# Two transformer blocks on one core: the first weight unit and x in two halves, constant matmuls at the start, one semaphore set for three FFNs

## The reference, cut to what matters

```python
def rms_norm(x, g):            # eps 1e-6
    return x * rsqrt(mean(x * x, axis=-1) + eps) * g

x = x + 0.5 * swiglu(rms_norm(x, ffn1_norm), ffn1_gate, ffn1_up, ffn1_down)
# swiglu(h, g, u, d) = (silu(h @ g) * (h @ u)) @ d, hidden width 2816
```

## Time and profile before

| | us |
|---|---|
| three runs | 1970.55, 1967.21, 1971.44 |
| their median | 1970.55 |
| the profiled execution | 1967.05 |
| its span, first to last instruction | 1965.3 |
| PE busy | 1926.3 |
| PE at the start of unit 0, of unit 2 | 14.27, 41.40 |

### The profile page before, as it was taken

One profiled execution on the slowest core, in us unless ns is written; L12 is line 12 of the kernel. 1 busy time (PEld: TensorE's weight loads), 2 busy tenths in 40 slices (PEclk: granted clock), 3 DMA queues, 4 the chain that ended last, 5 costly groups with the idle time before them and its releaser, 6 DMA issues.

```text
span 1965.3 us, 24117 instructions
## 1 busy us (share of the span) xinstructions
PE 1926.3 (98%) x9630; PEld 1558.6 (79%) x9630; DVE 907.5 (46%) x1182; ACT 705.2 (36%) x957; POOL 177.3 (9%) x150
## 2 busy tenths in 40 slices
PE   8999999999999999999999999999999979999998
PEld 6888888887778898888888878777677858888887
DVE  5444422447685654644442246343546454444313
ACT  5222221354534443423231143334545353222212
POOL 2000000204430200200000032000000030000000
PEclk9999999999999999999999999999999989999999
DMA  5333322332214223333323222221212313333322
GB/s 161 97 99 93 104 89 88 104 107 66 65 44 151 92 87 100 86 107 86 106 87 105 85 89 86 65 65 44 77 53 86 99 52 102 91 105 87 104 89 75
DMA packets 213697, 175.79 MB, mean 89 GB/s; under 512 B 6565, under 2 KB 201210, under 8 KB 213626
## 3 DMA queue, kind: packets, MB, share of 16 engines
q1 hardware_dynamic: 212928, 174.74, 29.0%
q10 hardware_dynamic: 698, 0.05, 0.0%
HBM read 172.67 MB, written 2.10 MB: 89 GB/s over the span
## 4 chain that ended last, share of the span: by engine, by line
PE 89%; DVE 4%; ACT 3%; POOL 2%; DMA 1%; issue 1%; SPq 0%; DVEq 0%; POOLq 0%; ACTq 0%
PE bank L484 25%; PE bank L486 24%; PE bank L485 24%; PE bank L658 6%; PE bank L531 2%; PE bank L951 1%; PE bank L532 1%; PE bank L533 1%; PE bank L920 1%; ACT w_hi L1049 1%; DVE w_lo L1511 1%; DMA w_raw<-in_w_in 1%; DVE n_lo L1520 1%; PE bank L935 1%; POOL hgrn_suffix L442 1%
## 5 line engine op out<-in xcount | busy, mean ns | idle before, releaser
L484 PE MATMUL bank<-n_hi,w_hi 128*128 128x512 f32 x1760 | 707.4, 402 | 18.5 <-DVE n_lo L1520 10.2
L1511 DVE TENSOR_TENSOR w_lo<-w_raw,w_hi 128x2048 fp32r<-128x2048 f32 x160 | 369.2, 2307 | 753.0 <-ACT w_hi L1049 752.9
L486 PE MATMUL bank<-n_hi,w_lo 128*128 128x512 f32 x1760 | 690.2, 392 | 0.0
L485 PE MATMUL bank<-n_lo,w_hi 128*128 128x512 f32 x1760 | 690.1, 392 | 0.0
L1049 ACT CAST w_hi<-w_raw 128x2048 fp32r<-128x2048 f32 x160 | 305.4, 1909 | 610.9 <-PE bank L486 526.0
L484 PEld LDWEIGHTS bank<-n_hi,w_hi 128*128 128x128 f32 x1760 | 332.9, 189 | 105.0 <-issue 23.6
L486 PEld LDWEIGHTS bank<-n_hi,w_lo 128*128 128x128 f32 x1760 | 333.0, 189 | 71.1
L485 PEld LDWEIGHTS bank<-n_lo,w_hi 128*128 128x128 f32 x1760 | 333.3, 189 | 67.6 <-issue 2.6
L425 POOL TENSOR_TENSOR sum_squares<-sum_squares,sq 128x512 f32<-128x512 f32 x42 | 66.0, 1571 | 933.2 <-ACT sq L1064 928.8
L484 PE MATMUL bank<-h_hi,w_hi 128*128 (+1 forms) x352 | 139.2, 396 | 0.0
L486 PE MATMUL bank<-h_hi,w_lo 128*128 (+1 forms) x352 | 139.1, 395 | 0.0
(11 more groups left out here) (306 smaller groups left out, 1954.6 us busy)
## 6 DMA issues: line engine op xcount, KB each, us to landing
w_raw<-in_w_in SPq DMA_DIRECT2D x68, 512.0 KB, 4.6
w_raw<-in_ffn_gate SPq DMA_DIRECT2D x44, 512.0 KB, 4.0
w_raw<-in_ffn_up SPq DMA_DIRECT2D x44, 512.0 KB, 5.2
w_raw<-in_ffn_down SPq DMA_DIRECT2D x44, 512.0 KB, 3.9
w_raw<-in_w_gate SPq DMA_DIRECT2D x22, 512.0 KB, 4.0
w_raw<-in_w_up SPq DMA_DIRECT2D x22, 512.0 KB, 5.2
w_raw<-in_w_down SPq DMA_DIRECT2D x22, 512.0 KB, 4.0
w_raw<-in_w_kv_mem SPq DMA_DIRECT2D x16, 512.0 KB, 4.5
```

Source lines behind the costliest of these rows:

```text
L484: pe.matmul(acc, w_hi, x_hi, start=start, stop=False)
L485: pe.matmul(acc, w_hi, x_lo, start=False, stop=False)
L486: return pe.matmul(acc, w_lo, x_hi, start=False, stop=stop)
L1511: dve.tensor_tensor(wlo[par][:, :], raw[par][:, :], whi[par][:, :].bitcast(F32), ALU.subtract).then_inc(w_lo_ready, 1)
```

## The change

What it does, all at the start except the last point:

- **Loads.** `x` comes in eight pieces (128 tokens by one half of the model dimension, 256 KB) and unit 0 in four (gate or up, four k chunks, 256 KB), each with its own semaphore. The order on SP: three pieces of the first half of `x`, gate, the fourth piece, up; then four pieces of the second half, gate, up. Then unit 1 as before.
- **Turning.** `turn_in(0)` turns chunks 0 to 3 into banks 4 to 7, `turn_in(1)` chunks 4 to 7 into banks 2 to 5; the two that reuse banks 4 and 5 wait for the copies of `x` out of them. `turn_in(1)` stands in PE's list behind unit 0's third k chunk.
- **Constant matmuls.** `warm(n)` multiplies ones by the identity into bank 0: six calls at the start, three behind the gain's transpose, three behind each of the four pieces of the first half.
- **Products.** Unit 0 goes k chunk by k chunk, gate then up, not all of gate first.
- **Splits.** ACT and DVE split unit 0 in four pieces of 512 columns, placed between the `n_hi` and `n_lo` of each half. DVE copies chunks 0 and 1 of `x` after four `n_lo`, the other six after all eight.
- **The sum.** In the first FFN the matmul that sums the squares stands behind unit 1's sixth k chunk, not its second.
- **Semaphores.** The three FFNs share six semaphores that count on (`h0` = 22 f is added to what is waited for), instead of six each.

```diff
+X_BANK = (4, 5, 6, 7, 2, 3, 4, 5)
@@ SP
-            for i in range(TT):
-                sp.dma_start(x_tok[:, i, :], xv[:, i, :]).then_inc(x_loaded[i], 16)
+            def load_first(half, g):
+                k0, at0 = 4 * half, (C * g + 4 * half) * P
+                sp.dma_start(raw[0][:, at0:at0 + 4 * P].rearrange("p (k n) -> p k n", k=4),
+                             first[g][:, k0:k0 + 4, 0:P]).then_inc(first_loaded[half][g], 16)
+
+            for half in range(2):
+                cols = slice(D // 2 * half, D // 2 * half + D // 2)
+                for i in range(TT):
+                    if i == TT - 1 and half == 0:
+                        load_first(half, 0)
+                    sp.dma_start(x_tok[:, i, cols], xv[:, i, cols]).then_inc(x_loaded[half][i], 16)
+                if half:
+                    load_first(half, 0)
+                load_first(half, 1)
@@ PE
-                    for g in range(2):
-                        if g == 0:
-                            pe.wait_ge(first_lo, 1)
-                        else:
-                            pe.wait_ge(w_lo_ready, 1)
-                        pe.wait_ge(x_ready, g + 1)
-                        for k in range(C):
-                            if g == 0:
-                                pe.wait_ge(n_ready, k + 1)
+                    for k in range(C):
+                        pe.wait_ge(n_ready, k + 1)
+                        for g in range(2):
+                            if k in (0, 4):
+                                pe.wait_ge(*((w_lo_ready, 1) if k and g else (first_lo, k // 2 + g + 1)))
...
+                        if k == 2:
+                            turn_in(1)
...
-                        else {1: lambda: sum_over_partitions(sums)})
+                        else {5 if f == 0 else 1: lambda: sum_over_partitions(sums)})
...
+            def warm(n):
+
+                for _ in range(n):
+                    pe.matmul(bank[0][:, 0:P], ones[:, :], ident[:, :], start=True, stop=True)
+
+            def turn_in(half):
+
+                for i in range(TT):
+                    pe.wait_ge(x_loaded[half][i], 16)
+                    for c in range(4 * half, 4 * half + 4):
+                        if i == 0 and c == 4:
+                            pe.wait_ge(gain1_ready, 1)
+                        if i == 0 and c > 5:
+                            pe.wait_ge(x_ready, c - 5)
+                        mm = pe.transpose(bank[X_BANK[c]][:, i * P:(i + 1) * P], x_tok[:, i, c * P:(c + 1) * P], ident[:, :])
+                        if i == TT - 1:
+                            mm.then_inc(x_turned, 1)
+                    if half == 0:
+                        warm(3)
+
             pe.wait_ge(ident_steps, 2)
+            warm(6)
             pe.wait_ge(gain1_loaded, 16)
...
+            warm(3)
+            turn_in(0)
@@ ACT
-            act.copy(whi[0][:, 0:W // 2], raw[0][:, 0:W // 2]).then_inc(first_hi, 1)
-            for c in range(C):
-                act.wait_ge(x_turned, c + 1)
-                act.activation(nhi[:, c, :], bank[c][:, :], ACT.Copy, scale=gain("ffn1_norm", c)).then_inc(n_hi_ready, 1)
-            act.wait_ge(w_loaded[0], 16)
-            act.copy(whi[0][:, W // 2:W], raw[0][:, W // 2:W]).then_inc(w_hi_ready, 1)
+            for half in range(2):
+                if half == 0:
+                    first_split(0, 0)
+                for c in range(4 * half, 4 * half + 4):
+                    if c in (1, 5):
+                        first_split(half, 1)
+                    act.wait_ge(x_turned, c + 1)
+                    act.activation(nhi[:, c, :], bank[X_BANK[c]][:, :], ACT.Copy, scale=gain("ffn1_norm", c)).then_inc(n_hi_ready, 1)
+                if half == 0:
+                    first_split(1, 0)
@@ DVE
+            for half in range(2):
+                if half == 0:
+                    first_split(0, 0)
+                for c in range(4 * half, 4 * half + 4):
+                    dve.wait_ge(n_hi_ready, c + 1)
+                    dve.scalar_tensor_tensor(nlo[:, c, :], bank[X_BANK[c]][:, :], gain("ffn1_norm", c), nhi[:, c, :].bitcast(F32),
+                                             ALU.mult, ALU.subtract).then_inc(n_ready, 1)
+                    if c in (0, 4):
+                        first_split(half, 1)
+                if half == 0:
+                    for c in range(2):
+                        keep_x(c)
+                    first_split(1, 0)
             for c in range(2, C):
-                dve.tensor_copy(x[:, c, :], bank[c][:, :]).then_inc(x_ready, 1)
+                keep_x(c)
             split_unit(1)
```

More of the change, by code:

```diff
@@ L233, in two_blocks @@
         unit_done = sem("unit_done")
-        x_loaded = [sem(f"x_loaded{i}") for i in range(TT)]
-        first_loaded, first_hi, first_lo = sem("first_loaded"), sem("first_hi"), sem("first_lo")
+        x_loaded = [[sem(f"x_loaded{half}_{i}") for i in range(TT)] for half in range(2)]
+        first_loaded = [[sem(f"first_loaded{half}_{g}") for g in range(2)] for half in range(2)]
+        first_hi, first_lo = sem("first_hi"), sem("first_lo")
         gain1_loaded, gains_loaded, taps_loaded = sem("gain1_loaded"), sem("gains_loaded"), sem("taps_loaded")
@@ L338, in gate_up @@
                     cols = bass.ds(n * P, P)
-                    load(par, [((0, W // 2, C), g[:, :, cols]), ((W // 2, W, C), p_[:, :, cols])],
-                         first_loaded if base == 0 and isinstance(n, int) and n == 0 else None)
+                    load(par, [((0, W // 2, C), g[:, :, cols]), ((W // 2, W, C), p_[:, :, cols])])
                 def down_pair(par, half, n):
@@ L345, in down_pair @@
                                ((W // 2, W, 1), d[:, bass.ds(2 * n + 1, 1), :])])
-                for j in range(2):
+                for j in range(1 if base == 0 else 0, 2):
                     gate_up((base + j) % 2, (base + j) // 2, j, base > 0)
@@ L676, in ffn_products @@
                     down(b + n, n, (b + n) % 2, last=(n == DOWN_UNITS - 1))
+            def warm(n):
[14 more added lines that the diff above has]
+                        warm(3)
             pe.wait_ge(ident_steps, 2)
+            warm(6)
             pe.wait_ge(gain1_loaded, 16)
-            pe.transpose(bank[7][:, 0:C], gain_rows[0:C, :], ident[0:C, 0:C]).then_inc(gain1_t, 1)
-            for i in range(TT):
-                pe.wait_ge(x_loaded[i], 16)
-                for c in range(C):
[L685 to L689, removed]
+            pe.transpose(bank[2][:, 0:C], gain_rows[0:C, :], ident[0:C, 0:C]).then_inc(gain1_t, 1)
+            warm(3)
+            turn_in(0)
             ffn_products(0, U_FFN1, N_FFN1, S_FFN1)
@@ L1043, in split @@
             def split(par, half, first=False):
-                act.wait_ge(w_loaded[par], 32 * half + (32 if par else 16))
+                act.wait_ge(w_loaded[par], 32 * half + (32 if par else 0))
                 if not first:
@@ L1146, in _, with first_split @@
             act.dma_start(convw[:, :, :], a["conv_w"][0].rearrange("(c p) j -> p c j", p=P)).then_inc(taps_loaded, 16)
+            def first_split(half, g):
+                cols = slice((C * g + 4 * half) * P, (C * g + 4 * half + 4) * P)
+                act.wait_ge(first_loaded[half][g], 16)
+                act.copy(whi[0][:, cols], raw[0][:, cols]).then_inc(w_hi_ready if half and g else first_hi, 1)
             act.wait_ge(gain1_ready, 1)
-            act.wait_ge(first_loaded, 16)
-            act.copy(whi[0][:, 0:W // 2], raw[0][:, 0:W // 2]).then_inc(first_hi, 1)
-            for c in range(C):
-                act.wait_ge(x_turned, c + 1)
-                act.activation(nhi[:, c, :], bank[c][:, :], ACT.Copy, scale=gain("ffn1_norm", c)).then_inc(n_hi_ready, 1)
-            act.wait_ge(w_loaded[0], 16)
-            act.copy(whi[0][:, W // 2:W], raw[0][:, W // 2:W]).then_inc(w_hi_ready, 1)
+            for half in range(2):
[8 more added lines that the diff above has]
+                    first_split(1, 0)
             split_unit(1)
@@ L1493, in _ @@
                     else:
[L1494 removed]
+                        act.wait_ge(down_done, 2 * (C - 1) + i + 1)
                     if i:
@@ L1616, in _, with first_split @@
-            dve.wait_ge(w_hi_ready, 1)
-            dve.tensor_tensor(wlo[0][:, W // 2:W], raw[0][:, W // 2:W], whi[0][:, W // 2:W].bitcast(F32),
-                              ALU.subtract).then_inc(w_lo_ready, 1)
+            def first_split(half, g):
+                cols = slice((C * g + 4 * half) * P, (C * g + 4 * half + 4) * P)
+                dve.wait_ge(*((w_hi_ready, 1) if half and g else (first_hi, 2 * half + g + 1)))
+                dve.tensor_tensor(wlo[0][:, cols], raw[0][:, cols], whi[0][:, cols].bitcast(F32),
+                                  ALU.subtract).then_inc(w_lo_ready if half and g else first_lo, 1)
```

70 lines of the change are left out of this document (31 added, 39 removed).

## The result

| | before | after |
|---|---|---|
| median, us (17 runs each) | 1967.21 | 1973.80 |
| lowest and highest, us | 1965.1, 1971.44 | 1970.99, 1976.03 |
| span of the profiled execution, us | 1965.3 | 1972.0 |

The ratio of after to before is 1.0029, with a 95% interval of 1.0022 to 1.0037: the change makes the kernel 0.29% slower, 5.7 us. The medians of all runs are further apart (6.6 us), the spans of the two profiles too (6.7); both still lie inside the interval, which is 4.3 to 7.3 us.

The account below looks back on a forecast made before the run. The PE's own work was taken to fill nine tenths of the span; unit 2's start 3.9 us later plus a second clock fall of 1.7 made 5.6, added to 1970.55 for 1976.2 us, range 1970 to 1980.

Parts of the forecast that it names:

- the start of unit 2: After unit 1 on the PE: unit 2 starts 7.94 us after the sum, 45.3 against 41.40, 3.9 us lost.
- the constant matmuls take it back: Before the first product: loads bring chunks 0 to 3 2 us earlier; 18 constant calls ahead of the last transposes cancel that.
- the first fall: Unit 1, behind the PE's new 3.4 us idle time: clock falls to half, costing 1.7 us before the sum.
- Unit 1's start: PE waits 3.4 us for DVE's split; unit 1 begins at 27.4 instead of 28.2, 0.8 us gained.
- Nothing behind gives it back: After unit 2's start: the loss stays to the end because the PE has no slack; total 5.6 us.
- the second fall: Unit 2, behind a 4.2 us wait: half clock again costs 1.7 us, or 3.05 with a long low stretch.
- The last rival: Start: clock does not rise in constant matmuls and transposes; 5.6 + 5.3 us lost, 1981.5; chance 0.05.
- rival 1: Early idle times: clock holds, sum at 35.6, unit 2 at 43.5, 2.1 us lost, 1972.7; chance 0.21.
- Rival 2: Start to sum: constant calls are one record, second half turned 2 us earlier, no change on balance, about 1970.5; chance 0.14.
- rival 3: End of unit 0: the 4.1 us gained pass through, unit 1 split by 24.0, faster at 1966.4; chance 0.04.

Follow-up runs that it names:

- version with both waits filled: Changed kernel plus 12 constant matmul calls ahead of unit 1 and 18 ahead of unit 2, in the PE's two new waits: 1972.99 us, ratio 1.0028.
- version rearranged: Changed kernel with early copies and squares of x, earlier splits of units 1 and 2, other banks, gain's transpose in unit 1: 1962.97 us, ratio 0.9980.

## Why the prediction was right

The forecast was 5.6 us slower, a median of 1976.2; measured are 5.7 us by the ratio and a median of 1973.8. The difference between 1976.2 and 1973.8 is in the base: the three runs shown before had a median of 1970.55, seventeen have 1967.21. That 5.6 and 5.7 agree so closely is luck, for the terms were each off, as the table and the points below show. By its own steps:

| step | predicted, us | profile of after |
|---|---|---|
| first product | 11.3 | 11.76 |
| second turning ends | 17.15 | about 17.7 |
| unit 1 split by DVE | 27.3 | 28.33 |
| POOL's first addition | 23.2 | 23.47 |
| sum's matmul, not waiting for POOL | 37.3 | 37.99 |
| unit 2 begins | 45.3 | 45.88 |
| idle ahead of unit 1, of unit 2 | 3.4, 4.2 | 3.2, 4.1 |

- **The chain.** That the gain at the first product would be lost on DVE, and that the start of unit 2 follows the sum by 7.9 us (here 45.88 - 37.99 = 7.9), is shown: cutting this tail alone takes the loss to where it can't be told from nothing (1.0006), and moving the sum alone brings most of it into the kernel before (1.0023). Without the constant matmuls the loss is the same, so the term "the constant matmuls take it back" is right for the timeline and is no cause of the loss.
- **What pays for what.** The prediction counted 3.9 us for the start of unit 2 as one sum. In the changed kernel the sum's place is worth 3.4 us by the ratios (1.0029 - 1.0012 = 0.0017 of 1967) and 4.1 by the medians, in the kernel before 4.6; all else together is the 1.7 to 2.4 us that are left with the sum back in its old place. I had not priced the two apart. The working held it (35.6 us for the PE against POOL's 35.0) and would have given the place of the sum 2.3 us at the sum itself (0.6 and the first fall, 35.0 against 37.3). The runs show something else: with the sum back, unit 2 begins only 0.2 us earlier (45.70 for 45.88), because the early sum's wait of 2.5 us and the half clock behind it keep the PE in unit 1 until then. What the late place costs is the wait of 4.1 us directly ahead of unit 2 and the half clock behind it: 13.7 us for unit 2 instead of 10.9.
- **Unit 1's start** was 1.0 us late on the forecast, in three parts. The first product was 0.46 late: the nine constant calls ahead of the first transposes took 0.48 us each (1.42 to 4.28, 4.48 to 5.92), not 0.43. The prediction's own sum for the second half's first `n_lo` is 0.15 short: 17.15 + 0.59 + 0.66 + 0.1 is 18.5, not 18.35. And DVE's subtraction for unit 1 was taken at 2.73 us and took 3.17. It begins inside an addition of POOL each time, and ends 2.15 us after that addition's end: 24.60 and 26.75 before, 26.18 and 28.33 here. These additions are (before, then after)

```profile
23.30 1.30 POOL L425 TENSOR_TENSOR sum_squares<-sum_squares,sq 128x512 f32<-128x512 f32 x1
```

```profile
24.92 1.26 POOL L440 TENSOR_TENSOR sum_squares<-sum_squares,sq 128x512 f32<-128x512 f32 x1
```

  So the longer time is a later end of the addition that it began in. Its price is not a constant that can be carried over.
- **The half clock** was the term that was mis-sized. The first fall was priced at 1.7 us, and the low stretch held 2.9 us of unit 1, 1.4 us. The second was priced at 1.7 with 3.05 as its upper bound; it held 5.8 us of unit 2, which took 13.7 us instead of 10.9, 2.8 us. In the profile unit 3 begins at 59.61 against 52.28, 7.3 us later: 4.5 for the start of unit 2 (3.9 forecast) and 2.8 for its clock. By the end 0.6 of it is given back, nearly all before 1300 us. DVE's subtraction for one and the same unit, at three places (before, then after):

```profile
65.35 2.29 DVE L1511 TENSOR_TENSOR w_lo<-w_raw,w_hi 128x2048 fp32r<-128x2048 f32 x1 [4.95 <-ACT w_hi L1049]
...
1300.82 2.29 DVE L1511 TENSOR_TENSOR w_lo<-w_raw,w_hi 128x2048 fp32r<-128x2048 f32 x1 [3.58 <-ACT w_hi L1049]
...
1938.75 2.29 DVE L1511 TENSOR_TENSOR w_lo<-w_raw,w_hi 128x2048 fp32r<-128x2048 f32 x1 [8.87 <-ACT w_hi L1049]
```

```profile
72.68 2.29 DVE L1547 TENSOR_TENSOR w_lo<-w_raw,w_hi 128x2048 fp32r<-128x2048 f32 x1 [4.95 <-ACT w_hi L1077]
...
1307.57 2.29 DVE L1547 TENSOR_TENSOR w_lo<-w_raw,w_hi 128x2048 fp32r<-128x2048 f32 x1 [3.58 <-ACT w_hi L1077]
...
1945.48 2.29 DVE L1547 TENSOR_TENSOR w_lo<-w_raw,w_hi 128x2048 fp32r<-128x2048 f32 x1 [8.86 <-ACT w_hi L1077]
```

  The distance is 7.33, 6.75 and 6.73 us, so the forecast's "Nothing behind gives it back" holds but for these 0.6. The price of the second fall is read from a pair of profiles alone. The version with both waits filled took it out of its profiles and didn't become faster in the median, so as a cost of the average execution this term is not shown. Executions of one kernel differ by more than it (5 us from lowest to highest).
- **The last rival,** that the clock would not rise ahead of the first product, fell: it rose at about 7.3 us, among transposes and constant matmuls in turn. The runs do not separate the two. With transposes alone in the changed kernel, in three pieces with waits between them, it rose only in the products, while in the kernel before, where all 32 transposes stand in a row, it rose within them. That it rose at the forecast moment is in part chance, since it came at other moments in other executions (last section).
- **The rivals.** The clock fell (rival 1 fell with it). Rival 2, nothing on balance, is outside the interval of the ratio. The version rearranged comes near what rival 3 asked for, unit 1 split by 24.0 (24.84 there): it wants the copies, squares and the split of unit 2 moved, none of which the change does.

## What to carry to other kernels

Before a start is quickened, follow what hangs on its *end*: here 2.5 us at the first product (14.27 to 11.76) were worth nothing, since everything up to the next unit stood behind the same seven microseconds of vector work, and a reduction moved four k chunks back, out of its wait, put 7.9 us of dependent work behind a later point. Move work that does not need the reduction's result ahead of the wait for it: here it cost nothing measurable where it wasn't needed (0.9996), and it cut the tail from 7.9 us to 4.6 where it was. And look in the windows for the half clock behind the waits of the matrix engine: in the profile of the changed kernel it made waits of 2.7 and 4.1 us dearer by 1.4 and 2.8 us.

## What the runs showed of the hardware that I had not expected

- **The moment of the clock's rise differs between executions of the same instructions.** The same six records of constant matmuls from 4.4 us on, in the changed kernel, in the one with unit 2 split ahead, with one constant matmul a piece, and in the rearranged one with one a piece:

```profile
4.48 1.65 PE L695 MATMUL bank<-ident,ones 128*128 128x128 f32 x6
```

```profile
4.48 1.52 PE L695 MATMUL bank<-ident,ones 128*128 128x128 f32 x6
```

```profile
4.48 1.21 PE L695 MATMUL bank<-ident,ones 128*128 128x128 f32 x6
```

```profile
4.44 0.94 PE L697 MATMUL bank<-ident,ones 128*128 128x128 f32 x6
```

  In the first they start 0.24 us apart and so run at half clock throughout; in the last they start 0.13 us apart, so the clock has risen before them or in their midst. In every one the PE's own instructions up to there are the same. So one profile's clock at the start is a sample.
- **A wait of about 2.5 us may or may not bring the clock down.** The one of 2.50 us with the sum back in its place was followed by half clock (the sum at 35.16, two records in 2.08 us), like the idle time of 1.70 us in the earlier trace rows; the waits of 0.82 us ahead of unit 2 were not. But in the kernel before with unit 2 split ahead, the wait of 2.40 us at the same place left the clock up, and the two records took 1.13 us:

```profile
32.10 1.13 PE L542 MATMUL bank<-sum_squares,ones 128*128 128x512 f32 x2 [2.40 <-POOL sum_squares L425]
```

  Late in the kernel the same holds for longer ones: behind 3.26 us of idle time at 1593 us the kernel before ran at half clock, and behind 3.30 us at 1600 the changed kernel ran on at full clock. These runs show both outcomes from 1.7 to 3.3 us, and no limit can be read from them. The waits of 4.1 us ahead of unit 2 brought it down in every profile that has one.
- **A subtraction on DVE and an addition on POOL take turns.** A subtraction that began inside an addition ended 2.15 us after the addition's end, and so took 2.73 us before and 3.17 in the changed kernel; in the rearranged one no addition runs when it begins, and it took 2.29. The addition issued in the meantime ended 1.1 us after the subtraction's end: 3.17 us long before, where the others took 1.31.
